# Two units of an attention output product moved ahead of the sample value up-projection, and that projection with its operands swapped, in a two-layer decoder step

## The reference, cut to what matters

```python
def mla_output(o_lat, w_uv, w_o):
    B, T = o_lat.shape[:2]
    o = jnp.einsum('bthc,chv->bthv', o_lat, w_uv).reshape(B, T, N_HEADS * V_HEAD)
    return o @ w_o
...
            m = mla_output(o_lat, W['w_uv'], W['w_o'][j])
        x = x + rms_norm(m, W['norm_mix_post'][i])
        h = rms_norm(x, W['norm_ff_pre'][i])
        x = x + rms_norm(sq_relu_mlp(h, W['w_up'][i], W['w_down'][i]), W['norm_ff_post'][i])
```

## Time and profile before

| | us |
|---|---|
| median of 3 runs | 1917.44 |
| lowest and highest | 1915.46 and 1927.88 |
| the profiled execution's own time | 1916.53 |
| its span, first to last instruction | 1914.4 |
| PE busy in it | 1782.8 (93%) |
| mean granted TensorE clock, share of full speed | 0.96 |

### The profile page before, as it was taken

How to read it: one execution, slowest core, us unless ns; L and a number is a source line. 1 busy time by engine, 2 the same in 40 slices (tenths; PEclk the granted TensorE clock), 3 DMA queues, 4 the chain that set the end, 5 groups by cost and what they waited for, 6 DMA issues and landing times.

```text
span 1914.4 us, 33398 instructions
## 1 busy us (share of the span) xinstructions
PE 1782.8 (93%) x12372; PEld 1605.6 (84%) x12372; DVE 920.4 (48%) x2169; ACT 737.9 (39%) x1457; POOL 1013.0 (53%) x737
## 2 busy tenths in 40 slices
PE   7987799989999999979899899999979999999978
PEld 6986799988999989879666465666969999999978
DVE  5896899844223256652444344442252222222383
ACT  5655444454444434432233333332332222223332
POOL 4993899967998975563111000001564555555562
PEclk9998899999999999989899899997979999999989
DMA  7331355533554523123003155555212222222201
GB/s 207 94 101 42 119 177 159 185 111 110 177 154 146 163 88 92 50 50 118 1 1 93 35 165 153 148 164 174 93 45 88 88 88 88 88 73 80 67 23 50
DMA packets 183289, 198.55 MB, mean 104 GB/s; under 512 B 32985, under 2 KB 138035, under 8 KB 183170
## 3 DMA queue, kind: packets, MB, share of 16 engines
q1 hardware_dynamic: 178414, 191.92, 32.4%
q10 hardware_dynamic: 4756, 5.04, 0.8%
HBM read 192.14 MB, written 4.79 MB: 103 GB/s over the span
## 4 chain that ended last, share of the span: by engine, by line
PE 71%; DVE 12%; POOL 10%; issue 3%; ACT 3%; DMA 1%; SPq 0%; ACTq 0%; POOLq 0%; DVEq 0%
PE bank L2340 18%; PE bank L2341 17%; PE bank L2342 17%; POOL WL L1328 6%; PE bank L2906 4%; PE bank L2940 3%; PE bank L2864 3%; DVE X L1657 2%; DVE AL L1625 2%; POOL acc L1354 1%; PE bank L2805 1%; DVE AL L1629 1%; PE bank L2786 1%; ACT WH L661 1%; POOL BL L1421 1%
## 5 line engine op out<-in xcount | busy, mean ns | idle before, releaser
L1328 POOL TENSOR_TENSOR WL<-RAW,WH 128x1024 fp32r<-128x1024 f32 (+1 forms) x281 | 666.2, 2380 | 678.5 <-ACT WH L661 676.7
L2340 PE MATMUL bank<-AH,WH 128*128 128x288 f32 x2112 | 646.0, 306 | 64.5 <-DVE AL L1625 31.3
L2341 PE MATMUL bank<-AL,WH 128*128 128x288 f32 x2112 | 633.6, 300 | 0.0
L2342 PE MATMUL bank<-AH,WL 128*128 128x288 f32 x2112 | 633.2, 300 | 0.0
L2340 PEld LDWEIGHTS bank<-AH,WH 128*128 128x128 f32 x2112 | 407.4, 193 | 80.0 <-DVE AL L1625 33.9
L2341 PEld LDWEIGHTS bank<-AL,WH 128*128 128x128 f32 x2112 | 407.9, 193 | 0.9
L2342 PEld LDWEIGHTS bank<-AH,WL 128*128 128x128 f32 x2112 | 407.3, 193 | 0.0
L661 ACT ACTIVATE WH<-RAW 128x1024 fp32r<-128x1024 f32 (+1 forms) x283 | 293.4, 1044 | 276.7 <-PE bank L2342 271.5
L2340 PE MATMUL bank<-BH,WH 128*128 128x288 f32 (+1 forms) x1120 | 337.7, 302 | 13.3 <-DVE S L1667 7.0
L2341 PE MATMUL bank<-BL,WH 128*128 128x288 f32 (+1 forms) x1120 | 334.8, 299 | 0.0
L2342 PE MATMUL bank<-BH,WL 128*128 128x288 f32 (+1 forms) x1120 | 334.6, 299 | 0.0
(11 more groups left out here) (271 smaller groups left out, 2128.8 us busy)
## 6 DMA issues: line engine op xcount, KB each, us to landing
RAW<-in_w_up SPq DMA_DIRECT2D x48, 1024.0 KB, 5.4
RAW<-in_w_down SPq DMA_DIRECT2D x48, 1024.0 KB, 5.0
RAW<-in_cache_kv_latent SPq DMA_DIRECT2D x128, 256.0 KB, 2.8
RAW<-in_conv_pw SPq DMA_DIRECT2D x16, 512.0 KB, 7.4
RAW<-in_conv_pw SPq DMA_DIRECT2D x8, 1024.0 KB, 5.0
RAW<-in_ple_gate SPq DMA_DIRECT2D x8, 1024.0 KB, 5.0
RAW<-in_cache_k_rope SPq DMA_DIRECT2D x128, 32.0 KB, 2.8
RAW<-in_w_o SPq DMA_DIRECT2D x4, 1024.0 KB, 4.9
```

What stands on the lines that cost most here:

```text
L1328: nc.gpsimd.tensor_tensor(split_part(WL, d, q), raw_part(d, q), split_part(WH, d, q).bitcast(F32), ALU.subtract).then_inc(lo_done, 1)
L2340: nc.tensor.matmul(out, wh, xh, start=first, stop=False)
L2341: nc.tensor.matmul(out, wh, xl, start=False, stop=False)
L2342: return nc.tensor.matmul(out, wl, xh, start=False, stop=last)
```

## The change

The list "wo" is cut into "wo" (slabs 0 and 1, tiles 0 to 3) and "wob" (slabs 2 and 3, tiles 4 to 7); the order of the 16 units stays. SP now loads the first two slabs of `w_o` ahead of `w_uv`, the other two behind it. ACT makes the first two parts of WH in the last step of the last sequence, between L1259 and the copy into SPT (L1268), and the next two right after the last `weigh`, without the wait for `keep`. On PE, unit 0 stands between `values` and `give`, unit 1 between `give` and the up-projection, unit 2 behind that, unit 3 behind four transposes, then the rest; these four units are of half 0. The up-projection has the 64 tokens of LATS as the stationary side and streams 128 columns of `w_uv`; two heads go to the lower and upper 64 rows of bank 4, alternating. ACT copies all of bank 4 into OUT in one instruction, PE turns OUT into bank 5 (four transposes), ACT copies that into AH at once, DVE puts the rest into AL at once. DVE copies units 0 to 2 out before that. In the sample attention the banks of the scores and of the values are exchanged (0 and 2).

```diff
-          ("uq", ...), ("kvh", ...), ("cache", 32, 0, 0, 8), ("uv", 2, CL // P, 0, 1), ("wo", 4, KT, 2, 1),
+          ("uq", ...), ("kvh", ...), ("cache", 32, 0, 0, 8), ("wo", 2, KT, 2, 1), ("uv", 2, CL // P, 0, 1),
+          ("wob", 2, KT, 2, 1),
...
             cache_loads(sp)
+            dense("wo", io["w_o"][0], KT, 256)
             for j in range(2):
                 g = RAW0["uv"] + j
...
-            dense("wo", io["w_o"][0], KT, 256)
+            dense("wob", io["w_o"][0], KT, 256, 2)
             sp.wait_ge(a_lo, A("o", 1, NH - 1))
...
                     nc.scalar.activation(col(ALPHA, j), nm(j - 1), ACT.Exp, scale=-1.0, bias=nm(j))\
                         .then_inc(exp_done, 1)
-                if not last:
+                if last:
+                    hi_next(2)
+                else:
                     for c in KEY_A:
                         key(c, j + 1 + 4 * i)
...
             weigh(NS - 1)
-            act.wait_ge(lat_out, 1 + NS)
             hi_next(2)
-            for hd in range(NH):
-                act.wait_ge(uv_mm, hd + 1)
-                nc.scalar.activation(AH[:, hd, TP:T], bank[hd % 4][:, 0:TS], ACT.Copy).then_inc(a_hi, 1)
-            hi_next(2)
+            act.wait_ge(uv_mm, NH)
+            nc.scalar.activation(OUT, bank[4][:, 0:512], ACT.Copy).then_inc(uv_natural, 1)
+            act.wait_ge(uv_turned, 1)
+            nc.scalar.activation(AH[:, :, TP:T], bank[5][:, 0:512].rearrange("p (h t) -> p h t", h=NH), ACT.Copy)\
+                .then_inc(a_hi, NH)
             after_mixer("y1", "ff1")
...
-                copy(0, 13)
+                copy(3, 13)
                 rstd(st, 0)
...
             keep(NS - 1)
-            for hd in range(NH):
-                dve.wait_ge(a_hi, A("o", 1, hd))
-                nc.vector.tensor_tensor(AL[:, hd, TP:T], bank[hd % 4][:, 0:TS], AH[:, hd, TP:T].bitcast(F32),
-                                        ALU.subtract).then_inc(a_lo, 1)
+            evacuate("wo", lambda h, m: half(Y, m, h), PAIRS, 0, 3)
+            dve.wait_ge(a_hi, A("o", 1, NH - 1))
+            nc.vector.tensor_tensor(AL[:, :, TP:T], bank[5][:, 0:512].rearrange("p (h t) -> p h t", h=NH),
+                                    AH[:, :, TP:T].bitcast(F32), ALU.subtract).then_inc(a_lo, NH)
             after_mixer("wo", "y1", "mix_post1", "ff1")
...
             values(3, NS - 1)
+            product("wo", None, 0, 1)
             give(NS - 1)
-
+            pe.wait_ge(swap_read, NS)
+            product("wo", None, 1, 2)
             pe.wait_ge(lat_out, 1 + NS)
-            for hd in range(NH):
-                g = RAW0["uv"] + hd // 4
-                if hd % 4 == 0:
+            for p in range(NH // 2):
+                g = RAW0["uv"] + p // 2
+                if p % 2 == 0:
                     pe.wait_ge(landed[g % RING], LANDED[g])
-                if hd >= 4:
-                    pe.wait_ge(a_lo, A("o", 1, hd - 4))
                 for k in range(4):
-                    a = k * 512 + (hd % 4) * P
-                    ins = nc.tensor.matmul(bank[hd % 4][:, 0:TS], RAW[:, g % RING, a:a + P],
-                                           LATS[:, k, hd].rearrange("p s t -> p (s t)"), start=k == 0, stop=k == 3)
-                ins.then_inc(uv_mm, 1)
+                    for hd in (2 * p, 2 * p + 1):
+                        a, rows64 = k * 512 + (hd % 4) * P, slice(64 * (hd % 2), 64 * (hd % 2) + 64)
+                        ins = nc.tensor.matmul(bank[4][rows64, p * P:(p + 1) * P],
+                                               LATS[:, k, hd].rearrange("p s t -> p (s t)"),
+                                               RAW[:, g % RING, a:a + P], start=k == 0, stop=k == 3)
+                        if k == 3:
+                            ins.then_inc(uv_mm, 1)
+            product("wo", None, 2, 3)
+            pe.wait_ge(uv_natural, 1)
+            for p in range(NH // 2):
+                ins = nc.tensor.transpose(bank[5][:, p * P:(p + 1) * P], OUT[:, p * P:(p + 1) * P], ident[:, :])
+            ins.then_inc(uv_turned, 1)
+            product("wo", None, 3, 4)
             pe.wait_ge(a_lo, A("o", 1, NH - 1))
-            product("wo", None, 0, 13)
+            product("wo", None, 4)
+            product("wob", None, 0, 5)
             total("y1", 0)
-            product("wo", None, 13, 16)
+            product("wob", None, 5)
             mlp(1)
```

More of the change, by code:

```diff
@@ L74 @@
           ("ple0", 1, 2, 8, 1), ("ffb", 4 * NCH, 0, 0, 1), ("gate0", 4, KT, 2, 1), ("dkv", 3, KT, 2, (1, 1, 2)), ("dq", 3, KT, 2, 1),
-          ("uq", 6, QL // P, 2, (2, 2, 2, 2, 4, 4)), ("kvh", 4, CL // P, 0, 2), ("cache", 32, 0, 0, 8), ("uv", 2, CL // P, 0, 1), ("wo", 4, KT, 2, 1),
+          ("uq", 6, QL // P, 2, (2, 2, 2, 2, 4, 4)), ("kvh", 4, CL // P, 0, 2), ("cache", 32, 0, 0, 8), ("wo", 2, KT, 2, 1), ("uv", 2, CL // P, 0, 1),
+          ("wob", 2, KT, 2, 1),
           ("mlp1", 4 * NCH, 0, 0, 1), ("ple1", 1, 2, 8, 1), ("gate1", 4, KT, 2, 1)]
@@ L119 @@
 GROUPS = {"pw1": [(j,) for j in range(8)], "ple0": [(0,)], "gate0": [(0, 1), (2, 3)],
-          "dkv": [(0, 1), (2,)], "dq": [(0,), (1, 2)], "uq": [(0, 1), (2, 3), (4, 5)], "wo": [(0, 1), (2, 3)],
+          "dkv": [(0, 1), (2,)], "dq": [(0,), (1, 2)], "uq": [(0, 1), (2, 3), (4, 5)], "wo": [(0, 1)], "wob": [(0, 1)],
           "ple1": [(0,)], "gate1": [(0, 1), (2, 3)]}
@@ L133 @@
 PAIRS, DKV, DQ, UQ = ([(h, 2 * j + t) for h, j, t in TILES[p]] for p in ("wo", "dkv", "dq", "uq"))
+PAIRS = PAIRS + [(h, m + 4) for h, m in PAIRS]
 def used_by():
@@ L361, in up_n @@
             return 4 * h + m
-        read_before = {"sw": "pw1", "kv": "gate0", "mx": "dkv", "cq": "dq", "ff1": "wo"}
+        read_before = {"sw": "pw1", "kv": "gate0", "mx": "dkv", "cq": "dq", "ff1": "wob"}
         gain_of = {"x0": "mix_pre0", "ff0": "ff_pre0", "g0": None, "kv": "kv_in", "mx": "mix_pre1",
@@ L396, in decoder_step @@
         dve_step, dup_set, seen, qsr_zero = sem("dve_step"), sem("dup_set"), sem("seen"), sem("qsr_zero")
+        uv_natural, uv_turned = sem("uv_natural"), sem("uv_turned")
         qrs_mm, qrs_c, uv_mm, y_turned, y_copied_v, y_copied_a = (sem("qrs_mm"), sem("qrs_c"), sem("uv_mm"),
@@ L444, in free, with dense @@
                 sp.wait_ge(lo_done, PART0[DENSE0[kind] + j + 1])
-            def dense(phase, w, kt, n):
+            def dense(phase, w, kt, n, first=0):
                 for j in range(SLABS[phase]):
@@ L451, in dense @@
                     sp.dma_start(slot(g, 0, kt * n).rearrange("p (k n) -> p k n", k=kt),
-                                 w.rearrange("(k p) n -> p k n", p=P)[:, :, j * n:(j + 1) * n])\
+                                 w.rearrange("(k p) n -> p k n", p=P)[:, :, (first + j) * n:(first + j + 1) * n])\
                         .then_inc(landed[g % RING], 16)
@@ L1252, in slab @@
                 act.wait_ge(sm_step, SM("bias", j) + NSM * i)
-                nc.scalar.activation(SP, bank[0][:, 0:256], ACT.Exp, scale=SCALE, bias=nm(j), accum_out=col(PSUMS, j))\
+                nc.scalar.activation(SP, bank[2][:, 0:256], ACT.Exp, scale=SCALE, bias=nm(j), accum_out=col(PSUMS, j))\
                     .then_inc(exp_done, 1)
@@ L2231, in slab @@
                 dve.wait_ge(score_mm, j + 2 + 4 * i)
-                step(nc.vector.tensor_reduce(col(TOP, j), bank[0][:, 0:256], AX.X, ALU.max))
+                step(nc.vector.tensor_reduce(col(TOP, j), bank[2][:, 0:256], AX.X, ALU.max))
                 dve.wait_ge(sm_step, SM("top", j) + NSM * i)
@@ L2255, in gain_output @@
                 if j == 0:
-                    nc.vector.tensor_copy(OUT, bank[2][:, :]).then_inc(out_done, 1)
+                    nc.vector.tensor_copy(OUT, bank[0][:, :]).then_inc(out_done, 1)
                 else:
                     dve.wait_ge(out_done, j + OUTS * i)
-                    nc.vector.scalar_tensor_tensor(out=OUT, in0=OUT, scalar=col(ALPHA, j), in1=bank[2][:, :],
+                    nc.vector.scalar_tensor_tensor(out=OUT, in0=OUT, scalar=col(ALPHA, j), in1=bank[0][:, :],
                                                    op0=ALU.mult, op1=ALU.add).then_inc(out_done, 1)
@@ L2905, in scores @@
                         q, k = (QS[:, c, :], KEYS[:, c, 256 * g:256 * g + 256]) if c < 4 else (QSR[:, g, :], ROPES)
-                        ins = nc.tensor.matmul(bank[0][64 * g:64 * g + 64, 0:256], q, k, start=c == 0, stop=c == 4)
+                        ins = nc.tensor.matmul(bank[2][64 * g:64 * g + 64, 0:256], q, k, start=c == 0, stop=c == 4)
                 ins.then_inc(score_mm, 1)
@@ L2929, in values @@
                     swap(i)
-                dst = [bank[2][64 * g:64 * g + 64, 0:512] for g in range(2)]
+                dst = [bank[0][64 * g:64 * g + 64, 0:512] for g in range(2)]
                 if j == 0:
```

## The result

The changed kernel took 1911.49 us in the median of 20 runs (1904.35 to 1920.67), the kernel before 1921.07 in 20 runs beside them (1914.71 to 1929.8). The ratio is 0.9942 with the 95% interval 0.9926 to 0.9958: 0.6% faster, some 11 us (8 to 14). Forecast were 12.6 us, a ratio of 0.9934. The median itself lies 6.7 us above the 1904.8 forecast, at the edge of the range (to 1911.5); 3.6 us of that are the kernel before, whose median was 1917.44 in the 3 runs shown and is 1921.07 in these 20. The profiled execution after took 1904.35 us, its span 1902.3 against 1914.4.

A forecast was written before the change was run, and what follows sets the result against it. PE bounds the kernel, losing time to waits, a slow up-projection and half clock. Counted along PE, the product's end moves from 1389.72 to 1377.15, 12.6 us: 1916.53 becomes 1903.9, plus 0.9 to the median gives 1904.8 us (1899.5 to 1911.5).

The forecast's parts named there:

- Early parts of WH: Two parts on ACT in the last step make the copy into SPT 1.4 us later, a cost on the path.
- Unit 0 in JOIN's wait, unit 1 in keep's: On PE, unit 0 follows the values product, ending 1321.45; unit 1 follows give, ending 1326.15, hiding DVE's keep.
- JOIN: Joining matrix: one stall to the end of POOL's third part (1321.6), JOIN at 1321.95, PE 0.5 us late.
- Up-projection: On PE, 64 instructions bound by 64-column loads at 0.070 us each: 4.5 us (2.2 to 7.0).
- the rival with the halves side by side: Up-projection halves run at once: pace 0.035, 2.2 us in all, time 1902.5 us; chance 0.07.
- The drain: TensorE draining at tiling-mode changes: some 0.3 us per switch, 0.4 us more in sum; set aside for 0.1 each.
- The turn: Four transposes on PE behind unit 2: 8 instructions at 0.109 us, 0.9 us, ending 1334.9.
- Copies under units 2 and 3, unit 4 without a wait: ACT's copies and DVE's rest hide under units 2 and 3; no wait of unit 4 for AL.
- The clock at the new wait: Rival: PE idle some 1.9 us, then units 0 and 1 at half clock; 1907 to 1915, typically 1909; chance 0.20.
- Behind the product: PE's idle for norm and AL moves along unchanged; rival: moved splits strike two more AL, 1910 us, chance 0.06.

The follow-up runs named there:

- shifted splits: Changed kernel with ACT waiting again for the kept result ahead of the third and fourth part of WH; one run, 1907.1 us, stretch 63.60 us.
- old operands: Changed kernel's order, but up-projection with 128x128 blocks of w_uv loaded and 64 tokens streamed, all heads into bank 4, no turn; ratio to before 0.9955.
- heads in turn: Changed kernel with the two heads of a pair one after the other instead of alternating in the up-projection; one run, 1915.11 us.
- neither edit: Old operands and all 16 units behind the up-projection, the change's load order, early parts of WH and joint copies kept; ratio to before 1.0024.

## Why the prediction was right, point by point

- *Early parts of WH*: +1.4 us forecast. The wait before the swap is 1.63 instead of 0.47: +1.16, undone by moving them one step earlier.
- *Unit 0 in JOIN's wait, unit 1 in keep's*: right. Unit 0 starts right behind the values product, unit 1 behind give, without a wait for weights.
- *JOIN*: I took one stall to the end of POOL's third split and PE 0.5 late. Three quarters of POOL's row (1315.67 + 0.75 x 9.37) end at 1322.70, JOIN at 1322.77, and PE waits 0.46. The shifted splits give the cause: JOIN 0.31 us without one beside it. The Trainium skill, "SBUF — State Buffer", section "SBUF: two separate sides", says that GpSimd and some forms of VectorE's instructions share a pair of ports as an exclusive lock held for a whole instruction; the rows agree.
- *Up-projection*: 4.5 us forecast from a load-bound row (0.070), 3.71 measured. The term was mis-sized, and its mechanism was wrong. Not the load is the bound but the stream: a half needs 0.109 us for 128 columns, and both halves stream at once, 0.058 an instruction. So the rival with the halves side by side was right in its mechanism and wrong in its price, since it halved the 0.070 of the load (0.035) instead of the 0.109 of the stream. I had set it aside by a row that I misread: that eight alternating instructions of 512 columns take 1.94 us doesn't show one stream after the other. In the kernel before, two instructions of 512 columns in one half alone (with 8 rows) take 1.07, so four times as many in 1.94 must share the time:

```profile
1299.78 1.07 PE L2933 MATMUL bank<-sq,root 8*64 8x512 f32 x2
```

- *The page on tiling*: the advice in the Trainium skill, "TensorEngine Tiling (Array Packing)", Performance Considerations, to swap and tile by columns pays here, from 0.113 to 0.058 each at full clock, with the streams in parallel. The drain that the page names at a change of mode costs less here than the 0.3 us that I had estimated: the up-projection starts 0.22 us after the last full-width instruction (1327.14 against 1326.92), where those start 0.13 apart, so some 0.09 more, the 0.1 of my sum.
- *The turn*: 8 instructions, 0.9 us forecast; it is four (a transpose of float32 data is one instruction here), with some 0.5 us on PE.
- *Copies under units 2 and 3, unit 4 without a wait*: right, no idle there.
- *The clock at the new wait* was the main rival. In the two profiles of the changed kernel it stayed full. In three of the others with the same 1.6 us wait and a dense unit behind it (old operands, heads in turn, late splits) it fell right behind it for some 3 us (with the heads in turn 0.50 in 1326.60 to 1329.90) and was back before the up-projection; that is about 1 us in the stretch, where I had priced 2.5 to 10.5. So it was luck, as far as these profiles tell, that it stayed full in the two. With a wait of 0.47 it stayed full in all three.
- *Behind the product*: carried through, as said; no further AL was struck.

The forecast of 12.6 us for the profiled execution stands against 12.1 in the span and 13.5 in the stretch, since its last factor came 1.1 us later. In the stretch the forecast was 0.9 us too long (1377.15 - 1313.56 = 63.59 against 62.68), of which the up-projection alone is 0.8; what the other terms were off nearly cancels.

## What to carry to other kernels

When a chain of small steps leaves PE waiting, put units that depend on none of them between the links: they fill the waits, and here the clock stayed full or was back before the up-projection. A matmul with few streamed columns behind a full-width load can count as busy and still stay at half clock for its whole length; with the operands swapped the same product is shorter and lets the clock come back. Two column halves of TensorE stream at the same time when instructions for one and the other alternate (0.058 us each against 0.071 four tiles at a time). Place a large POOL instruction where no DVE instruction of the chain stands beside it, but look for what waits for the moved one.

## What the runs showed that I had not expected

The old up-projection keeps whichever clock it finds: 13.9 us at half with PE always counted busy, before and with neither edit, and 7.25 us at full behind dense units. In the swapped form, with all units behind, the clock rose from half to full under it (0.50, then 0.96).

Even an instruction of two elements a row is held up by POOL: the statistics copy took 0.68 us instead of 0.16, up to the end of the first split (1315.67 + 9.37/4 = 1318.01, the copy 1318.04). The tiny scalings of JOIN's chain beside the same splits kept their 0.2 to 0.3 us.

The last factor's time varies by 10 us between profiles of kernels that are nearly alike up to there, as much as the whole gain. Timed ratios need many runs for effects of this size; a stretch between two named instructions repeats within 0.02 us (62.68 and 62.67, 60.82 and 60.83). By the DVE instructions, taken in their order, the profiles lie within 4 us of each other at 950 us of the span and 11 us apart at 1075, ahead of the sample attention; from there on they keep their distance. In that part the granted clock differs too: in 985.20 to 991.00 it is 1.00 in the profiles before and after, and 0.50 with the heads in turn. Which of the two comes first stays open.
